# The masked score products of a chunked recurrence, one chunk of 64 tokens at a time instead of one tile of 128

## The reference, cut to what matters

```python
CHUNK = 64
mask = jnp.tril(jnp.ones((CHUNK, CHUNK), dtype=bool))

def step(S, inp):
    qc, kc, vc, gc = inp
    b = jnp.cumsum(gc, axis=1)
    b_ref = b[:, CHUNK // 2 - 1][:, None]
    b_last = b[:, -1]
    o_inter = jnp.einsum('bchk,bhkv->bchv', qc * jnp.exp(b), S)
    A = jnp.einsum('bthk,bshk->bhts', qc * jnp.exp(b - b_ref), kc * jnp.exp(b_ref - b))
    A = jnp.where(mask, A, 0.0)
    o_intra = jnp.einsum('bhts,bshv->bthv', A, vc)
    S_new = jnp.exp(b_last)[..., None] * S + jnp.einsum(
        'bshk,bshv->bhkv', kc * jnp.exp(b_last[:, None] - b), vc)
    return S_new, o_inter + o_intra
```

## The time and the profile before

| what | us |
|---|---|
| median of three runs | 2609.81 (2609.26 to 2611.46) |
| the profiled execution's own time | 2609.81 |
| its span from first to last instruction | 2607.9 |
| PE busy | 2469.4 (95%) |
| PE weight loads busy | 2018.8 (77%) |
| DVE busy | 1327.0 (51%) |
| POOL busy | 883.0 (34%) |
| ACT busy | 795.5 (31%) |

### The profile page before, as it was taken

One profiled execution on the slowest core, in us unless ns is written; L12 is line 12 of the kernel. 1 busy time (PEld: TensorE's weight loads), 2 busy tenths in 40 slices (PEclk: granted clock), 3 DMA queues, 4 the chain that ended last, 5 costly groups with the idle time before them and its releaser, 6 DMA issues.

```text
span 2607.9 us, 30678 instructions
## 1 busy us (share of the span) xinstructions
PE 2469.4 (95%) x12985; PEld 2018.8 (77%) x12985; DVE 1327.0 (51%) x1704; ACT 795.5 (31%) x1083; POOL 883.0 (34%) x633
## 2 busy tenths in 40 slices
PE   7999899999999999898999999989999988999998
PEld 4888778888888888687777778878886437888886
DVE  2898765645444344876566655564651224211113
ACT  2322661311111112326531222234432333222212
POOL 2006002233233232462034554534442003444442
PEclk9898999999999999899999999989998999999999
DMA  8332103224443332221044554621104001233331
GB/s 264 97 97 84 64 1 114 81 81 129 122 137 92 120 104 83 73 91 57 1 115 144 150 171 143 182 81 49 49 17 129 0 0 49 78 100 97 90 97 57
DMA packets 309225, 240.57 MB, mean 92 GB/s; under 512 B 10692, under 2 KB 304831, under 8 KB 309087
## 3 DMA queue, kind: packets, MB, share of 16 engines
q1 hardware_dynamic: 308674, 238.47, 30.1%
q10 hardware_dynamic: 414, 0.13, 0.0%
HBM read 232.29 MB, written 2.10 MB: 90 GB/s over the span
## 4 chain that ended last, share of the span: by engine, by line
PE 85%; DVE 9%; ACT 3%; DMA 1%; issue 1%; POOL 0%; SPq 0%; DVEq 0%; ACTq 0%
PE ps L2496 61%; PE ps L1148 5%; PE ps L721 2%; DVE mod_w L2128 2%; PE ps L2531 2%; PE ps L934 2%; DVE mod_ctx L2128 1%; PE ps L1168 1%; PE ps L672 1%; PE ps L2411 1%; PE ps L2448 1%; PE ps L748 1%; PE ps L896 1%; DVE small L1038 1%; ACT probs L978 1%
## 5 line engine op out<-in xcount | busy, mean ns | idle before, releaser
L1634 POOL TENSOR_TENSOR w_lo<-raw,w_hi 128x512 fp32r<-128x512 f32 x518 | 756.1, 1490 | 1408.6 <-ACT w_hi L1742 1408.5
L2496 PE MATMUL ps<-h_hi,w_hi 128*128 128x512 f32 x1994 | 648.7, 371 | 25.5 <-DVE h_lo L2092 21.4
L2496 PE MATMUL ps<-h_lo,w_hi 128*128 128x512 f32 x1994 | 639.0, 366 | 0.0
L2496 PE MATMUL ps<-h_hi,w_lo 128*128 128x512 f32 x1994 | 638.0, 366 | 0.0
L1742 ACT ACTIVATE w_hi<-raw 128x2048 fp32r<-128x2048 f32 (+2 forms) x155 | 264.8, 1709 | 596.1 <-PE ps L2496 366.0
L2496 PEld LDWEIGHTS ps<-h_hi,w_hi 128*128 128x128 f32 x1994 | 339.9, 190 | 94.2 <-issue 23.4
L2496 PEld LDWEIGHTS ps<-h_hi,w_lo 128*128 128x128 f32 x1994 | 339.4, 190 | 66.9
L2496 PEld LDWEIGHTS ps<-h_lo,w_hi 128*128 128x128 f32 x1994 | 340.0, 190 | 65.7 <-issue 0.2
L2019 ACT ACTIVATE xg<-ps 128x512 f32<-128x512 f32 (+1 forms) x66 | 44.2, 670 | 677.1 <-PE ps L2496 490.6
L2128 DVE SCALAR_TENSOR_TENSOR mod_w<-mod_w,cond 128x512 f32<-128x512 f32 x224 | 240.8, 1075 | 3.4
L2496 PE MATMUL ps<-hid_hi,w_hi 128*128 128x512 f32 x704 | 232.1, 370 | 0.0
(11 more groups left out here) (368 smaller groups left out, 3220.9 us busy)
## 6 DMA issues: line engine op xcount, KB each, us to landing
mod_w<-in_w_mod SPq DMA_DIRECT2D x72, 1024.0 KB, 9.4
raw<-in_w_ffn_in SPq DMA_DIRECT2D x88, 512.0 KB, 5.2
raw<-in_w_in SPq DMA_DIRECT2D x54, 512.0 KB, 4.8
raw<-in_w_ffn_out SPq DMA_DIRECT2D x48, 384.0 KB, 3.8
raw<-in_w_out SPq DMA_DIRECT2D x24, 512.0 KB, 4.6
raw<-in_w_gate SPq DMA_DIRECT2D x22, 512.0 KB, 4.0
raw<-in_w_up SPq DMA_DIRECT2D x22, 512.0 KB, 5.4
raw<-in_w_down SPq DMA_DIRECT2D x24, 384.0 KB, 3.8
```

Source lines behind the costliest of these rows:

```text
L1634: ins = pool.tensor_tensor(w_lo[:, s, at:end], raw[:, s, at:end], w_hi[:, s, at:end].bitcast(F32), ALU.subtract)
L2496: ins = pe.matmul(ps[0:m, at:at + tw], weight(part, k, cols), v[:, held[k] if held else k, t0:t0 + tw], start=(at_k == 0 and j == 0 and no ...
```

## The change

The loop over four tiles of 128 tokens becomes a loop over eight chunks of 64. For a chunk there are two matmuls: its 64 keys against its 32 late queries, and 32 early keys against 32 early queries. Keys of a chunk are no longer multiplied with the queries of its neighbour. The odd chunks' scores stand in partitions 64 to 127 as before, but in the same 64 columns as the even ones', so the scores of an element take 256 columns of PSUM instead of 512, and DVE's source is 256 columns without a stride.

```diff
                 mid = CHUNK // 2
                 early, late = (0, mid) if d == 0 else (mid, 0)
-                for t in range(LAT // P):
-                    at = A_AT + P * t
-                    to = ps[:, at:at + P].rearrange("p (c q) -> p c q", q=CHUNK)
-                    q = at_token(g_q2[d], P * t, P).rearrange("p (c q) -> p c q", q=CHUNK)
-                    pe.matmul(to[:, :, late:late + mid], at_token(g_k[d], P * t, P), q[:, :, late:late + mid], start=True, stop=True)
-                    for first in (early, CHUNK + early):
-                        ins = pe.matmul(ps[first:first + mid, at + first:at + first + mid],
-                                        at_token(g_k[d], P * t + first, mid), at_token(g_q2[d], P * t + first, mid),
+                for c in range(NCH_LAT):
+                    row, at = CHUNK * (c % 2), A_AT + CHUNK * (c // 2)
+                    for q0, k0, kw in ((late, 0, CHUNK), (early, early, mid)):
+                        ins = pe.matmul(ps[row + k0:row + k0 + kw, at + q0:at + q0 + mid],
+                                        at_token(g_k[d], CHUNK * c + k0, kw), at_token(g_q2[d], CHUNK * c + q0, mid),
                                         start=True, stop=True)
                 ins.then_inc(g_a, 1)
...
                     ins = dve.copy_predicated(g_masked[rows, d, :].rearrange("p (t s) -> p t s", s=P)[:, :, cols], mask,
-                                              ps[rows, A_AT:A_AT + LAT].rearrange("p (t s) -> p t s", s=P)[:, :, cols])
+                                              ps[rows, A_AT:A_AT + 256].rearrange("p (t s) -> p t s", s=CHUNK))
                 ins.then_inc(g_am, 1)
```

## The result

The changed kernel takes 2625.68 us (median of 7 runs, 2618.03 to 2629.70), against 2610.90 for the kernel before on the same chip (7 runs, 2604.87 to 2613.20): a ratio of 1.0059, 95% interval 1.0048 to 1.0070, or 15.4 us more (the two medians alone differ by 14.8). It is slower, as forecast, but by more than the 9.0 us forecast, and 0.7 us above the range of 2613 to 2625. The two intervals only just overlap; the profiles show how much is the change's own.

A forecast was written before the change was run, and what follows sets the result against it. PE was taken to bound the kernel in elements 0 to 6; 1.28 us more of score products in each gives 7 x 1.28 = 9.0, and 2609.8 + 9.0 = 2618.8 us, range 2613 to 2625.

The forecast's parts named there:

- PE is the chain: In the third layer's projection, PE's score products are paid in full for elements 0 to 6: 7 x 1.28 = 9.0 us.
- Wide group 0.23, narrow 0.18, entry 0.20, element 1.28: Score products: us per 64-wide group, per 32-wide group, for entering after the transposes, and added per element in all.
- The step that no row had shown: Score products: going from 64 to 32 wide drains the array, taken from the Trainium skill's rule on tiling modes.
- The 16 switches: Width changes in an element's score products, 15 inside and one on leaving, each paid; inner ones in the group prices.
- Element 7 hidden: Last element: its 1.28 us more fit into PE's 3.89 us wait behind a weight transfer and cost nothing.
- DVE: Score copies out of PSUM: number unchanged, 0.90 us for two, scores still early, so they cost nothing.
- The clock falls: Rival: the longer, emptier keys stretch lowers PE's clock, up to 3 us a fall; one or two give 2620 to 2625; chance 0.06.
- a clock of 0.50 between 1800 and 1960 us: Sign in the changed profile, over the elements' stretch, that would show the prediction wrong.
- The rival without a gap: Score products: widths follow without draining; with array halves side by side 2601.2 us (chance 0.06), without overlap 2605.7 (0.05).

The follow-up runs named there:

- the orders: Three kernels with only the order of widths changed, two from the changed kernel, one from the kernel before: ratios 0.9966, 0.9975 and 0.9983 to the kernel before.
- the second interval: The changed kernel measured again on another chip against the kernel before: ratio 1.0037 (1.0023 to 1.0052), 9.7 us more.
- split: Changed kernel with each element's score products in two halves, the second some twelve block matmuls later: ratio 1.0036 to the kernel before, 9.4 us more.
- twice: Changed kernel with all eight chunks' score products made twice: ratio 1.0233 to the kernel before, 60.9 us more.
- sparse10: Kernel before with ten tiles' score products for an element instead of four: ratio 1.0109 to the kernel before, 28.5 us more.
- sparse: Kernel before with three of four tiles' score products made twice: ratio 1.0037 to the kernel before, 9.7 us more.
- grouped64: Changed kernel with its loops exchanged, an element's eight 64-wide groups first, then the eight 32-wide: ratio 0.9966 to the kernel before, 8.9 us less.
- dense: Kernel before with 1.28 us of block-like matmuls added ahead of each element's score products: ratio 1.0042 to the kernel before, 11.0 us more.
- after3: The changed kernel a third time, unaltered, for another profile: 2627.53 us in one run.

## Why the prediction was right in its sign and wrong in its size

1. *PE is the chain.* Right: the 1.28 us of seven elements are in the stretch in full, also when they are put there as dense matmuls (9.25 for 9.0).
2. *Wide group 0.23, narrow 0.18, entry 0.20, element 1.28.* Right to 0.01 each. The step that no row had shown, a drain between 64 and 32, was as taken, and the orders show its price: 0.12 us for a switch, 0.20 where it also parts two chunks. (The 16 switches that the prediction counts between 64 and 32 are 15 and the one from 32 to 128 on leaving; the sum has them right.) The rule of the Trainium skill ("TensorEngine Tiling (Array Packing)", Key Properties), that a change of mode drains the engine, agrees with that.
3. *Element 7 hidden.* Right: a wait of 3.59 us is left behind it. I had said 2.6. From the end of the one-column matmuls to the last block matmul ahead of the wait PE took 11.3 us before (1967.35 to 1978.64) and 11.4 after (1984.68 to 1996.05): before, all twelve block matmuls ahead of element 7 stood at half clock, 0.43 us apart, and after only the last eight of them, which made up for most of the longer products. What the forecast left out is that the one-column matmuls ahead of it decide when the transfer starts: by another fall of the clock they gave 2.0 us back.
4. *DVE.* Right: the copies take 0.43 to 0.46 us as before, and PE waited for none.
5. *The clock falls.* This is the step that failed: it was named as a rival, with 0.06, and left out of the sum, and its own sign, a clock of 0.50 between 1800 and 1960 us, came true. The stretch shows 167.88 - 153.91 = 13.97 us. The widths are 8.96. The block matmuls behind elements 1, 2 and 5 took 8.62, 7.99 and 6.64 us instead of 7.06, 6.37 and 5.09: 1.56 + 1.62 + 1.55 = 4.7, and 13.7 together. The other 0.3 lie in the blocks behind elements 4 and 6, at full clock: many of their matmuls start 0.118 us apart where they started 0.114 apart before. Behind element 6, before and after:

```profile
1943.21 5.66 PE ps L1148 x45
...
1962.38 5.84 PE ps L1148 x45
```

The price of a fall was in reach from the earlier trace rows, as half its length. Its likelihood was not worked out. I had the one comparison, 2.9 us without a fall, and took it to speak against one at 4.1 us. It said nothing of 4.1 us, and the three profiles have three falls each. Nor was it "after 6.4 us" of one-column matmuls that the clock fell: a mean of 0.71 over 7 us is 4.1 us at 0.50, so it fell near 1962.9, 2.0 us into them. That row spoke for a fall, and was read as if it spoke of a far longer piece. The range also stopped at 2625 where its own sum gave 2625.5; the measured 2625.7 is outside both.
6. *The rival without a gap.* Refuted between the two widths, but half of it is right and worth having: matmuls of one width do overlap in distinct columns of the array (0.96 us for 32). Its gain needs an order in which the width stays the same. What the Trainium skill says of concurrent column groups ("TensorE: Matmul & The Clock Gate", Part 3) holds here with that condition.

Of the 15.4 us of the first comparison 11.8 are read off the profiles up to the wait behind element 7; where the rest arises isn't shown, and the start of element 0 alone differs by 4 us between the two profiles of the kernel before. 11.8 us are 0.45%: inside the second interval (0.23 to 0.52%) and just below the first (0.48 to 0.70%). The 9.7 us measured on the other chip lie near the forecast's 9.0, but that is luck: the forecast had neither the 4.7 us of the falls nor the 2.2 that come back.

What stays open: what exactly brings the clock down. With dense matmuls between the halves of an element there was no fall (split), more of the same small groups brought more falls (twice, sparse10), and groups with wider loads and more moving columns stood 4.5 us without one (sparse), each in one profile. With the one-column matmuls a fall came 2.0 us after the first of them in the kernel before, and 5.2 us after it in the changed one. Which elements are hit differs between executions of one kernel. Open too is what sets the spacing of the block matmuls at full clock, 0.114 or 0.118 us, with no wait in the profile. It is why grouped64 saved 6.4 us in the stretch where its products alone save 7 x (2.00 - 0.96) = 7.3: the block behind element 1 takes 7.25 instead of 7.06, and all seven together 0.8 more. The 9.25 of dense above 9.0 are of this kind too.

## What to carry to other kernels

Small matmuls of different stationary widths should be sorted by width, not by the tile of data they belong to: here a switch cost 0.12 us, and 0.20 where it also kept two matmuls from running side by side in different columns, and sorting alone turned a loss of 14.0 us in the stretch into a gain of 6.4. An edit that lengthens or thins out a piece of small matmuls is to be priced with the clock in the block behind it, and where a term like that can't be excluded by a row of at least the new length, it belongs in the sum's range with real weight. For an effect of half a per cent, look for a stretch between two landmarks that holds the change and nothing else: it was steady to 0.2 us where whole executions scattered over 10. Then look at one landmark more: here 2.2 of the 14.0 us came back right behind the stretch.

## What the runs showed of the hardware that was not expected

- Two profiles of the same kernel differ by 4 us before any changed instruction (element 0 at 1803.09 and 1807.05), with the same work; the kernels here span 1803 to 1813 at that point.
- In the changed kernel the fall of the clock comes in the dense matmuls behind the sparse piece, and hardly in it: 3.28 us of products at 1.00, then 3.4 us of block matmuls at 0.50 (in after3 one fall begins 0.6 us before the products end). The loss is booked on lines that nobody edited.
- The moment of a fall moves as well: the same forty one-column matmuls took 6.39 us with a fall 2.0 us into them and 4.37 with none.
- Thirty-two loads and matmuls of 64 and 32 columns in 0.96 us: 0.03 us from start to start on average, where two 64-wide loads in the same columns start 0.055 apart or more.
